# A drain on the pool engine behind the two gathers of every row

## The reference, cut to what matters

```
idx = take_along_axis(cand_i, pos)            # tokens x 8 heads x 16
g   = softmax(top_s)
u   = u_tab[idx]                              # gather, 1024 wide
act = gelu(einsum('thkd,td->thk', u, hb))
v   = v_tab[idx]                              # gather, 1024 wide
out = einsum('thk,thkd->td', g * act, v)
```

## Time and profile before

| | us |
|---|---|
| median of 3 runs | 2387.41 |
| lowest and highest | 2378.56, 2394.47 |
| span of the profiled execution (no other time is given for it) | 2379.3 |

### The profile page before, as it was taken

How to read it: one execution, slowest core, us unless ns; L and a number is a source line. 1 busy time by engine, 2 the same in 40 slices (tenths; PEclk the granted TensorE clock), 3 DMA queues, 4 the chain that set the end, 5 groups by cost and what they waited for, 6 DMA issues and landing times.

```text
span 2379.3 us, 27257 instructions
## 1 busy us (share of the span) xinstructions
PE 2070.6 (87%) x9038; PEld 1171.1 (49%) x9039; DVE 979.9 (41%) x2276; ACT 555.0 (23%) x1027; POOL 497.6 (21%) x562
## 2 busy tenths in 40 slices
PE   8998998967658576584999989999999999999998
PEld 7867887623223232232678854444444444444443
DVE  5955555646647566473375232111111111111112
ACT  4636301212112111122214222211111111121112
POOL 0000003466666666665300000000000000000000
PEclk9999999988878787896999989999999999999999
DMA  7352586799999999998842428799999999999996
GB/s 301 142 212 80 195 356 262 277 368 344 370 380 344 366 364 353 371 345 327 345 180 107 176 97 372 301 429 429 428 428 428 430 428 428 429 429 428 428 429 280
DMA packets 111703, 784.34 MB, mean 330 GB/s; under 512 B 13056, under 2 KB 13312, under 8 KB 80160
## 3 DMA queue, kind: packets, MB, share of 16 engines
q1 hardware_dynamic: 37920, 515.18, 52.3%
q0 software_dynamic: 73728, 268.47, 29.8%
HBM read 782.55 MB, written 1.05 MB: 329 GB/s over the span
## 4 chain that ended last, share of the span: by engine, by line
PE 75%; issue 11%; DVE 5%; another core or an unknown queue 2%; ACT 2%; POOL 2%; DMA 1%; DVEq 0%; ACTq 0%; POOLq 0%; SPq 0%
PE ps L786 56%; PE ps L945 16%; PE ps L1210 1%; DVE ring L1942 1%; DVE arena L1942 1%; DMA arena<-in_peer_v,arena 1%; PE ps L918 1%; POOL ring L746 1%; POOL ring L744 1%; DMA ring<-in_peer_v,arena 1%; DVE arena L1700 0%; DVE arena L1891 0%; ACT arena L1372 0%; PE ps L1241 0%
## 5 line engine op out<-in xcount | busy, mean ns | idle before, releaser
L786 PE MATMUL ps<-ring,arena 128*64 128x512 f32 (+2 forms) x3336 | 749.5, 589 | 41.8 <-issue 41.7
L786 PEld LDWEIGHTS ps<-ring,arena 128*64 128x64 f32 (+1 forms) x3336 | 262.9, 140 | 501.5 <-issue 500.7
L945 PE MATMUL ps<-ring,arena 128*128 128x512 f32 x768 | 366.5, 635 | 156.8 <-issue 134.7
L786 PE MATMUL ps<-arena,ring 128*128 128x256 f32 (+1 forms) x2272 | 486.2, 373 | 3.8 <-DVE arena L1685 3.2
L786 PEld LDWEIGHTS ps<-arena,ring 128*128 128x128 f32 x2272 | 417.4, 189 | 65.5 <-issue 6.9
L945 PEld LDWEIGHTS ps<-ring,arena 128*128 128x128 f32 x768 | 154.9, 204 | 364.6 <-issue 340.0
L945 PE MATMUL ps<-arena 128*128 128x512 f32 (+2 forms) x600 | 211.3, 599 | 66.5 <-ACT arena L1278 50.6
L1942 DVE CUSTOM_DVE_ANT_0 ring<-ring,ps 128x1024 f32<-128x1024 f32 x192 | 228.1, 1218 | 94.8 <-DMA ring<-in_peer_v,arena 88.5
L1600 ACT COPY arena<-ps 128x512 f32<-128x512 f32 (+1 forms) x165 | 89.2, 541 | 739.6 <-PE ps L786 683.5
L2255 DVE TENSOR_TENSOR arena<-ps,arena 128x512 f32<-128x512 f32 x66 | 45.7, 692 | 438.4 <-PE ps L1210 438.4
L786 PE MATMUL ps<-arena 128*128 128x128 f32 (+4 forms) x1502 | 215.2, 298 | 11.1 <-ACT arena L1262 6.6
(11 more groups left out here) (336 smaller groups left out, 1214.5 us busy)
## 6 DMA issues: line engine op xcount, KB each, us to landing
ring<-in_w_exp SPq DMA_DIRECT2D x192, 2048.0 KB, 17.1
ring<-in_w_in SPq DMA_DIRECT2D x24, 2048.0 KB, 9.5
ring<-in_w_ada SPq DMA_DIRECT2D x12, 2048.0 KB, 8.8
ring<-in_w_out SPq DMA_DIRECT2D x4, 2048.0 KB, 8.2
ring<-in_w_peer_q SPq DMA_DIRECT2D x4, 2048.0 KB, 10.6
ring<-in_w_br_rnn SPq DMA_DIRECT2D x4, 1280.0 KB, 7.4
ring<-in_w_br_attn SPq DMA_DIRECT2D x2, 2048.0 KB, 13.9
ring<-in_peer_u,arena POOLq DMA_INDIRECT x192
```

The source lines that it names most:

```text
L786: return pe.matmul(o, l, r, start=start, stop=stop)
L945: return pe.matmul(o, l, r, start=start, stop=False, skip_group_check=True)
```

## The change

POOL executes a drain behind the second gather of every row, 256 times in all. A drain holds up the engine's own instruction stream; it waits for no semaphore and sets none.

```diff
                             pool.indirect_dma_start(out=uv_rows[k][:, D:2 * D], out_offset=None, in_=a["peer_v"],
                                                     in_offset=at_k).then_inc(uv_full[k], 16)
+                            pool.drain()
                 own.leave(PH // 2)
```

## The result

The kernel with the drain takes **3533.8 us** (median of 4 runs, 3529.1 to 3537.4) against 2387.7 us of the kernel before in the same group: a ratio of 1.480, 95% interval 1.476 to 1.484, or +1146 us. The profiled execution has a span of 3527.2 us against 2379.3, +1147.9.

A forecast was written before the change was run, and what follows sets the result against it. The prediction took the expert-table loop from gather to freed row as the bound, POOL near its own pace. Rows of 6.4 + 0.97 = 7.37 us against 2.92 add 1120 us: span 3499, median 3507 us, range 3310 to 3700.

The forecast's parts named there:

- Issue to landing: Expert-table stage, each row: first gather's start to the dot that waited for that row, 6.4 us, 2.18 us of it issuing.
- Restart: POOL, from a finished drain to the next row's first gather: 0.97 us, in place of the 0.30 us visible before.
- The rows with the copy: Every 16th row, where POOL copies indices before gathering: 15 copies of some 0.4 us each on top of 7.37 us.
- The last dot: End of the expert-table stage: the last row's dot starts at 2278.4 us instead of 1158.8, so the stage ends 1120 us later.
- The DMA engines at a third of their time: Sign expected in the changed profile's expert-table stage: DMA engines busy a third of the time, at about 140 GB/s.
- No wait for `s_pv`: Sign expected in the changed profile: POOL no longer waits for used rows, where it had waited 94 us.
- The likeliest case: Each drain on POOL waits until both gathers of its row have landed: +1120 us, 3507 us, chance 80%.
- rival 1: The drain waits for POOL alone, not the landing; gap before each row about 1.0 us: +67 us, 2454 us, chance 9%.
- 2 (every drain 7.58): Every drain costs like the one at the program's end; rows of 10.73 us: +1976 us, 4364 us, chance 4%.
- 4 (nothing): The 256 drains cost only the 8 to 10 ns of idle engines' drains, 2 us in all: 2389 us, chance 3%.
- 3: Faster: a pause per row ends DVE's stand-stills and POOL's 94 us of waits; 2305 us at 0.05 us a row, chance 4%.
- POOL's own 94 us of waits vanish inside the sum: Expert-table stage: POOL's 94 us of waits for used rows disappear within the longer rows rather than adding to them.

## Why the prediction was right

**The sum**, 3507 against 3533.8, span 3499 against 3527.2, term by term:

- Issue to landing, taken as 6.4 us: the dot starts 6.47 us behind the first gather in the median, the drain ends at 6.57. Some 0.1 us belongs to the drain itself: with the plain wait in its place the row is 7.34 us instead of 7.46.
- Restart, taken as 0.97: 0.89. The row is 7.46 in the median and 7.47 in the mean against 7.37; 240 rows, +24 us.
- The rows with the copy, taken as 7.77: 8.21 in the mean, since the copy itself now stands behind a restart; 15 of them, +7 us. 255 rows take 1916.0 us against the 1885 of the sum.
- The last dot starts at 2309.4 instead of 2278.4, +1150.6 to before. Its last products end 0.7 us sooner than before behind it, and the third stage is 2 us shorter: the +1147.9 of the spans. Nothing of the 30 us is elsewhere.

**What was said of the profile.** Drains of some 4 us: 4.37 behind the gathers, though the bar says 6.29. First gathers 7 to 8 us apart: yes. 142 GB/s: 140 in the stage. The DMA engines at a third of their time: 0.44, wrong; their share fell less (0.92 to 0.44) than the rate (347 to 140). A dot behind each landing: 254 of 256. No wait for `s_pv`: the list of waits names PE's product for 31 of POOL's 255 gaps,

```profile
POOL ring L744 <- issue: 817.9, 155, 7.3
...
POOL ring L744 <- PE ps L946: 114.0, 22, 6.1
```

but these are 5.2 us each like those with no releaser (5.3): a product ended inside the gap, and the drain is what filled it. Not foreseen: the mean granted clock fell from 0.84 to 0.66 in the stage, where PE was busy 649 of 1929 us instead of 548 of 780, and PE's busy time rose by 101 us. It cost nothing, as PE still waited for ACT's diagonals (it idled 928 us for them ahead of the largest group of products).

**The reason given was weaker than the forecast.** The likeliest case leaned on the 7.58 us drain of the earlier trace rows: "there is more behind it", and of what a gather leaves behind, I took the transfer. But that drain began at 1390.0 and the last dot, which needs the last gather, at 1158.8. Everything had landed 230 us before, so the row could not show a wait for a landing, and the single drain at 1073.4 shows that it is work on gathers already done. That POOL's drain waits for the landing was true, but no row of the kernel before could tell it from rival 1. The halved gathers, the second drain of 41 ns and the plain wait show it. With what the rows really bore, rival 1 deserved more than 9%, and that the right one of the two was taken as the likeliest was in part luck. The Trainium skill, PSUM — Partial Sum Buffer, Engine vs sequencer instructions, lets a drain wait until the engine is fully idle; read strictly that was rival 1, and for POOL with gathers the runs make "idle" include the landing. The Trainium skill's Perfetto Trace Analysis, Per-engine timelines, puts a gather's shown end at its last descriptor and counts a drain's bar from the start of its execution. The trace agrees with the first (4.37 us between shown end and drain end); on the second it shows that the bar begins 0.27 us behind the start of the first gather.

**The rivals.** 1 (+67 us): out, by 256 drains of 4.4 us behind POOL's last instruction. 2 (every drain 7.58): out, the second of two takes 41 ns. 4 (nothing): out. 3 had a true half: with the drain DVE's stand-stills are gone, and 97 us with them, against 1243 us for it. That this half had a real price was also in my step "POOL's own 94 us of waits vanish inside the sum", which held. That POOL and DVE meet at a shared port was not shown: in the other groups POOL issues faster still (rows of 2.55 us) and DVE never stands still.

## What to carry to other kernels

A drain on the engine that issues gathers is a wait for their landing and a restart, about 4.4 + 0.9 us here against 0.3, so its price is the overlap that it takes away. The pause is the time from the last gather's end on its engine to the landing, with as many gathers in flight as there will be, and the restart less the usual gap: 4.4 + 0.9 - 0.3 = 5.0 us here behind two gathers, some 6.6 behind eight. It counts once for every drain. The drain's own price is 0.1 us. If a landing must be awaited, wait some rows behind: with three rows in flight the kernel loses 2%, with two 13%, with one (the drain, beside a kernel before of 2290 us) 54%. And before a long bar is read as a wait for something, look when that something ended.

## What the hardware showed beside that

- A drain on POOL takes 0.04 us with nothing since the last one, 7.58 us at the first drain behind 512 landed gathers of 4 KB or of 2 KB rows, and this work is off the path there (ratio 1.000).
- Gathers of 2 KB rows take POOL as long as those of 4 KB (0.946 and 0.938 us).
- In groups without stand-stills the gathers arrive at 408 GB/s with a DMA share of 1.03 and rows of 2.55 us, just over POOL's 2.49. With half the bytes the share is 0.71 and the rows are 2.58 us: a full DMA share does not show that the transfers are the limit.
- The same program takes 4% longer in one group than in another with one stage alone affected, together with DVE's drains of up to 16 us. A drain on POOL every four rows, a pause of 7 us, ended them; whether by the pause or by the emptied queue was not tried. The cause is open.
